# Keeping one expert pass in SBUF in place of two: the pass ahead of the last goes to DRAM by a scatter

## The chip, the cores and the metric

The kernel runs on one core of one Trainium2 chip. The metric is the device time of one launch in microseconds (us). The core has a matrix engine (PE, TensorE), a vector engine (DVE, VectorE), a scalar engine (ACT, ScalarE), GpSimd (POOL) and a queue engine (SP, SyncE); DMAs are issued from SP, ACT and POOL and share 16 DMA engines.

## What is computed

One inference step of a decoder layer for 512 prompt tokens and 8 sample tokens, 1024 wide. A pooling and mLSTM mixer and a cross-attention come first. The change concerns only the last step, a mixture of 16 gated-MLP experts, two for each token, and the last layer norm:

```python
hg = jnp.einsum('nd,edf->nef', xf, p['w_gate'])
hu = jnp.einsum('nd,edf->nef', xf, p['w_up'])
hh = jax.nn.silu(hg) * hu * combine[..., None]
y = jnp.einsum('nef,efd->nd', hh, p['w_down'])
...
x = layer_norm(ALPHA * x + hier_moe(x, p), p['ln3_g'], p['ln3_b'])
```

`combine` has two nonzero entries for each token (top expert group, then the top two of its four experts), so 520 tokens make 1040 rows of expert work.

## The kernel before

**Passes.** The 1040 rows are sorted by expert into 12 passes (`NPASS`) of 128 slots. Three experts (`FIRST`) have a pass each; the other 13 are ordered by their count of tokens, the fullest first, and share nine passes in groups of 32 slots. A slot holds a token's number, its gate and the row of `y_d` to which its result belongs (`entry(p)`). With the given inputs the counts leave 109, 95, 60, 98, 87 and 59 used slots in passes 6 to 11 (counted from the reference's routing and the table `GROUPS`).

**One pass.** POOL gathers the rows of its tokens from DRAM, PE turns them (L1125), multiplies by gate and up weights (L1144), turns the hidden rows (L1151) and multiplies by the down weights (L1164). DVE and ACT scale the two halves of the result by the gate and write it to `ysb`, a ring of three slots (DVE L2571, ACT L1749). PE's stream is laid so that the down products of pass p-1 come behind the gate and up products of pass p. SP streams the weights.

**Where a result goes.** For the first `NSCAT` = 10 passes POOL then scatters the 128 rows to `y_d` in DRAM by an indirect DMA (`scatter`, L2921). `y_d` has two halves, one for each token's first choice and one for its second. The last `KEPT` = 2 passes, 10 and 11, are not scattered: DVE builds for each a 0/1 matrix `places` of slots against tokens (`place_rows`, L2577 to L2581), and PE multiplies it with `ysb` (`add_kept` L1182 for the prompt, `add_samples` L1186 for the samples), so that the sums stand in PSUM by token.

**The end.** When all scatters have landed (`y_out`), POOL adds the rows of `y_d` to the residual `xn` by accumulating DMAs: `accumulate` (L2958) for the first choice of the samples and of prompt tiles 0, 1 and 2, then, behind waits, the second choice of the samples, the first of tile 4, and the second of tiles 2 and 4. SP loads the second choice of tiles 0 and 1 plainly into a weight buffer (L1352), and DVE adds it (L2598, two adds, ahead of everything that follows on DVE), each when its tile's two transfers have landed. Then DVE walks over the tiles in the order 0, samples, 1, 2, 4 (`LAST_NORM`): it adds the PSUM sums of the kept passes (L2625, two halves), takes the mean (L2630) and centres (L2632); ACT takes the squares and scales (L1784 to L1790), and POOL sends the tile out by an accumulating DMA (L2974). The last tile is finished by DVE (L2643) and sent by SP and ACT (L1358, L1793).

Every engine works its stream in order. What holds the scatters back from the accumulates is this wait on POOL, and the same on SP ahead of L1352:

```python
for i in range(3):
    pool.wait_ge(y_out[i], 16 * SCATTERS[i])
```

In the rows below `P` is the large SBUF buffer in which `ysb`, the centred tiles and others lie, `smp` holds `places` and the slot lists, `wring` and `mkT`/`mv` are weight buffers, and `ps` is PSUM.

Of the kernel before, what the change touches and what calls it, by code (L numbers as in the profile page):

```python
# [67 lines left out]
NSORT = NE - NFULL  # L68
RELEASE = [max(p for p in range(NPASS) if any(part[0] == n for part in PASS[p])) for n in range(NE)]
KCOL = NPASS - NFULL  # L70
KEPT = 2
NSCAT = NPASS - KEPT
SCATTERS = [len(range(i, NSCAT, 3)) for i in range(3)]
LW = 3
# [52 lines left out]
def layer_kernel(nc, a, o):  # L127
# [3 lines left out]
    with ctx:  # L131
# [3 lines left out]
        def sem(name):  # L135
            return ctx.enter_context(nc.semaphore(name))
# [46 lines left out]
        ps = [ctx.enter_context(nc.psum_tensor(f"ps{i}", [128, 512], F32)) for i in range(8)]  # L183
# [5 lines left out]
        def view(lo, n, pat=None, **kw):  # L189
            v = P[:, lo:lo + n]  # L190
            return v.rearrange(pat, **kw) if pat else v
# [83 lines left out]
        zeros = view(16094, 256)  # L275
        places = smp[:, 1120:1120 + KEPT * NTOK].rearrange("p (i c) -> p i c", i=KEPT)
        tokens16 = smp[:, 2162:2162 + KEPT]
        squares = view(10464, D)
# [3 lines left out]
        kept_bank = lambda t, q: 2 * PROMPT.index(t) + q  # L282
# [91 lines left out]
        y_act, y_dve = sem("y_act"), sem("y_dve")  # L374
        y_out = [sem(f"y_out{i}") for i in range(3)]
        sum_full, row_parts = sem("sum_full"), sem("row_parts")
# [21 lines left out]
        def wcols(w, c0, n=512):  # L398
# [8 lines left out]
                  ("wq0", wcols(a["ca_wq"], 0)), ("wq1", wcols(a["ca_wq"], 512)),  # L407
                  ("wc0", wcols(a["ca_wo"], 0)), ("wc1", wcols(a["ca_wo"], 512))]
        BI = {name: i for i, (name, _) in enumerate(BLOCKS)}
        NB = len(BLOCKS)  # L410
        assert NB % WR == 0
# [76 lines left out]
        def _(pe):  # L488
# [692 lines left out]
            def add_kept(i, bank, t, q, **open_close):  # L1181
                return mm(bank[:, :], places[:, i, START[t]:START[t] + TR], ysb[:, (NSCAT + i) % 3, q * 512:q * 512 + 512], **open_close)  # L1182

            def add_samples(i, bank):
                for g in range(4):
                    last = mm(bank[32 * g:32 * g + NS, 0:256], places[:, i, NP_:NTOK], ysb[:, (NSCAT + i) % 3, g * 256:g * 256 + 256],  # L1186
                              start=(i == 0), stop=(i == KEPT - 1))
                return last

            pe.wait_ge(places_ready, KEPT)  # L1190
            pe.wait_ge(y_act, NSCAT + 1)
            pe.wait_ge(y_dve, NSCAT + 1)
            add_samples(0, ps[6])
            add_kept(0, ps[0], 0, 0, start=True, stop=False)
            pe.wait_ge(y_act, NPASS)
            pe.wait_ge(y_dve, NPASS)
            for t in PROMPT:
                if t == 4:
                    pe.wait_ge(y_act, NPASS + 1)
                    pe.wait_ge(y_dve, NPASS + 1)  # L1200
                for q in range(2):
                    bank = ps[kept_bank(t, q)]
                    if (t, q) != (0, 0):
                        add_kept(0, bank, t, q, start=True, stop=False)
                    add_kept(1, bank, t, q, start=False, stop=True).then_inc(sum_full, 1)
                if t == 0:
                    add_samples(1, ps[6]).then_inc(sum_full, 1)

            with pe.If(over > 0):
                with pe.Fori(0, NE) as e:  # L1210
# [603 lines left out]
        def _(dve):  # L1814
# [749 lines left out]
            def expert_out(p):  # L2564
                dve.wait_ge(y_full, p + 1)
                if p >= 3:
                    dve.wait_ge(y_out[p % 3], 16 * (p // 3))
                elif p == 2:
                    dve.wait_ge(c_out, 32)
                dve.wait_ge(*entry_landed(p))  # L2570
                V.tensor_scalar(ysb[:, p % 3, 512:D], ps[5][:, :], entry(p)[:, 1:2], None, ALU.mult).then_inc(y_dve, 1)  # L2571

            def place_rows(i):
                p = NSCAT + i
                dve.wait_ge(*entry_landed(p))
                number = tokens16[:, i:i + 1]
                link(V.tensor_copy(number, entry(p)[:, 0:1].bitcast(U32)))  # L2577
                link(V.tensor_scalar(number, number, float(NE), None, ALU.mult))
                for t in range(NT):
                    n = rows_of(t)  # L2580
                    last = V.tensor_scalar(places[:, i, START[t]:START[t] + n], slots16[:, 0:n], number, -float(NE * START[t]), ALU.subtract, ALU.is_equal)  # L2581
                last.then_inc(places_ready, 1)

            for p in range(NPASS):
# [5 lines left out]
                if p > 0:  # L2590
                    expert_out(p - 1)
                if NPASS - 4 <= p < NPASS - 4 + KEPT:
                    place_rows(p - NPASS + 4)
# [426 lines left out]
```

## Time and profile before

| | us |
|---|---|
| median of 3 runs (lowest, highest) | 658.12 (658.09, 659.34) |
| the profiled execution | 657.6 |
| its span, first to last instruction | 655.9 |
| passes 9 to 11, each | about 11.7, the last shorter |
| result of the last scattered pass (9) in SBUF | at 612.94 |
| its scatter landed | at 618.90 |
| result of pass 10, of pass 11 in SBUF | at 624.44, 629.31 |
| first add of the last norm on DVE | at 632.51 |

Times "at" are microseconds from the start of the span. What stands outside the span is 657.6 - 655.9 = 1.7 us. The rows are read as a chain: the instruction that ended last, what released it, and so back. Busy shares alone (PE 95%) do not tell what the end of the program waits for.

### The profile page before, as it was taken

What the parts mean: (1) busy time and instruction counts of PE and PEld (TensorE: products, weight loads), DVE (VectorE), ACT (ScalarE), POOL (GpSimd) and SP (SyncE); (2) the same over time, 40 slices, a digit from 0 to 9 for tenths busy, and PEclk for the clock granted to TensorE, in tenths of its full rate; (3) what the DMA queues carried; (4) which work ended last, traced back from release to release, by engine and by line L of the source; (5) the groups of instructions that cost most, each with busy time, mean ns of one, the idle gap of its engine ahead of it and who ended that gap; (6) DMA issues with size and microseconds to landing.
All of it is one profiled execution on the core that took longest, in us unless ns stands there. A gap on an engine that the chain in (4) does not pass through costs nothing.

```text
span 655.9 us, 8866 instructions
## 1 busy us (share of the span) xinstructions
PE 625.2 (95%) x3279; PEld 399.9 (61%) x3279; DVE 365.5 (56%) x832; ACT 166.2 (25%) x371; POOL 205.7 (31%) x249
## 2 busy tenths in 40 slices
PE   6999999999999979999999999999999999999992
PEld 3588788887788844447888764454664454333330
DVE  1576797327646844557544865356864233253466
ACT  1184301102553120002003630223414111211144
POOL 7140100101667645212003983103234432111221
PEclk9999999999999989999999999999999999999997
DMA  8994588706355244005606886557638999999797
GB/s 280 364 371 139 191 196 233 252 2 210 115 164 193 94 176 146 16 1 205 243 6 230 327 270 262 224 204 282 253 126 352 415 411 415 403 375 414 271 178 158
DMA packets 49430, 150.29 MB, mean 229 GB/s; under 512 B 5691, under 2 KB 8459, under 8 KB 45153
## 3 DMA queue, kind: packets, MB, share of 16 engines
q1 hardware_dynamic: 35159, 112.48, 45.7%
q0 software_dynamic: 11488, 31.97, 17.2%
q10 hardware_dynamic: 2738, 5.23, 2.1%
q8 instruction: 28, 0.46, 0.3%
q14 instruction: 17, 0.14, 0.1%
HBM read 132.38 MB, written 22.43 MB: 236 GB/s over the span
## 4 chain that ended last, share of the span: by engine, by line
PE 77%; DMA 8%; DVE 7%; ACT 2%; POOL 2%; SPq 2%; issue 2%; DVEq 0%; POOLq 0%; ACTq 0%
PE ps L610 14%; PE ps L787 14%; PE ps L1144 12%; PE ps L608 7%; PE ps L516 5%; PE ps L1164 5%; DMA xn<-in_x_sample 2%; PE ps L806 2%; PE ps L889 2%; DMA xn<-y_d 2%; PE ps L1125 1%; PE ps L873 1%; PE ps L1016 1%; PE ps L583 1%; DMA wring<-in_ca_wq 1%
## 5 line engine op out<-in xcount | busy, mean ns | idle before, releaser
L787 PE MATMUL ps<-wring,P 128*128 128x512 f32 x224 | 99.2, 596 | 0.0
L787 PEld LDWEIGHTS ps<-wring,P 128*128 128x128 f32 x224 | 41.6, 190 | 49.1 <-issue 49.0
L1916 DVE SCALAR_TENSOR_TENSOR P<-ps,P 128x256 f32<-128x256 f32 (+1 forms) x83 | 33.7, 424 | 57.3 <-PE ps L610 36.6
L1144 PE MATMUL ps<-wring,P 128*32 128x512 f32 (+1 forms) x288 | 63.6, 593 | 0.9 <-DVE P L2549 0.9
L516 PE MATMUL ps<-xT,wring 128*128 128x312 f32 (+1 forms) x256 | 57.4, 383 | 0.0
L516 PEld LDWEIGHTS ps<-xT,wring 128*128 128x128 f32 x256 | 46.4, 190 | 9.3
L2549 DVE COPY P<-ps 128x512 f32<-128x512 f32 x11 | 7.6, 692 | 73.5 <-PE ps L1125 73.5
L1144 PEld LDWEIGHTS ps<-wring,P 128*32 128x32 f32 (+1 forms) x288 | 21.6, 128 | 35.0 <-issue 34.9
L2723 POOL TENSOR_SCALAR rstd<-agg 128x1 f32<-128x1 f32 (+1 forms) x10 | 12.0, 1196 | 88.0 <-DVE agg L1846 88.0
L2871 POOL TENSOR_TENSOR P<-P,xT 128x2048 f32<-128x2048 f32 x8 | 36.1, 4524 | 9.0 <-DMA xT<-sq_d 5.2
L2224 DVE SCALAR_TENSOR_TENSOR xn<-xn,ps 128x512 f32<-128x512 f32 x16 | 11.0, 685 | 44.9 <-PE ps L787 32.0
L1164 PE MATMUL ps<-P 128*32 128x512 f32 (+1 forms) x144 | 32.6, 594 | 0.6 <-issue 0.6
L608 PE MATMUL ps<-wring,P 128*128 128x256 f32 x128 | 29.5, 380 | 1.2 <-DVE wring L1891 1.2
L610 PE MATMUL ps<-xT,wring 128*128 128x264 f32 (+1 forms) x128 | 29.7, 387 | 0.2 <-DMA wring<-in_ca_wq 0.2
L610 PE MATMUL ps<-P 128*128 128x264 f32 x128 | 29.5, 385 | 0.0
L610 PE MATMUL ps<-P,wring 128*128 128x256 f32 (+1 forms) x128 | 29.2, 382 | 0.0
L1144 PE MATMUL ps<-xT,P 128*32 128x512 f32 (+1 forms) x96 | 28.2, 593 | 0.0
L610 PEld LDWEIGHTS ps<-xT,wring 128*128 128x128 f32 x128 | 23.8, 190 | 5.1 <-issue 1.1
L608 PEld LDWEIGHTS ps<-wring,P 128*128 128x128 f32 x128 | 23.8, 190 | 5.0 <-DVE wring L1891 1.6
L610 PEld LDWEIGHTS ps<-P 128*128 128x128 f32 x128 | 24.3, 190 | 4.2
L1469 ACT ACTIVATE xT<-ps 128x512 f32<-128x512 f32 (+1 forms) x20 | 9.5, 515 | 67.4 <-PE ps L583 67.3
L610 PEld LDWEIGHTS ps<-P,wring 128*128 128x128 f32 x128 | 24.2, 190 | 3.8
(464 smaller groups left out, 1171.6 us busy)
## 6 DMA issues: line engine op xcount, KB each, us to landing
wring<-in_w_in SPq DMA_DIRECT2D x5, 2048.0 KB, 9.8
wring<-in_w_gate SPq DMA_DIRECT2D x10, 1024.0 KB, 8.8
wring<-in_w_up SPq DMA_DIRECT2D x10, 1024.0 KB, 12.7
P<-in_w_down SPq DMA_DIRECT2D x10, 1024.0 KB, 13.5
P<-in_cache_mem_k SPq DMA_DIRECT2D x8, 1024.0 KB, 7.0
P<-in_cache_mem_v SPq DMA_DIRECT2D x8, 1024.0 KB, 6.1
y_d<-P POOLq DMA_DIRECT2D x1, 4160.0 KB, 31.6
wring<-in_ca_wv SPq DMA_DIRECT2D x2, 2048.0 KB, 20.4
```

The source lines that it names most:

```text
L516: last = mm(out, lhs(k), rhs(k), start=(k == 0), stop=(k == n - 1))
L608: last = mm(bank[:, 0:n], x[:, k, 128 * i:128 * i + 128], w[:, k, :], start=(k == 0), stop=(k == 3))
L610: last = mm(bank[:, 0:n], w[:, k, 128 * i:128 * i + 128], x[:, k, :], start=(k == 0), stop=(k == 3))
L787: last = mm(bk[:, :], src[:, k, START[t]:START[t] + TR], w[:, k, :], start=(k == 0), stop=(k == KC - 1))
L806: last = mm(bank[:, :], mixT[:, k, 0:TR], w[:, k, :], start=(k == 4), stop=(k == 1))
L889: last = mm(bk[:, 0:cn], mv[:, m, h * CE + ec * 128:h * CE + ec * 128 + 128], paT[:, h, m, c0:c0 + cn], start=(m == 0), stop=(m == 1))
L1144: last = mm(GU[p % 2][lo:lo + m, :].rearrange("p (g f) -> p g f", g=2), xgT[:, p % 3, k, lo:lo + m], gu[s][:, :, k, :], start=(k == 0), st ...
L1164: last = mm(YB[q][lo:lo + m, :], hT[:, p % 2, f, lo:lo + m], dn[s][:, f, q * 512:q * 512 + 512], start=(f == 0), stop=(f == 1))
L1916: V.scalar_tensor_tensor(dst, src, scale, part, ALU.mult, ALU.add).then_inc(part_added, 1)
L2224: V.scalar_tensor_tensor(x, x, ALPHA, bk[:, :], ALU.mult, ALU.add).then_inc(dve_free, 1)
L2723: link(G.tensor_scalar(x, agg[0:n, 1:2], LN_EPS, None, ALU.add))
L2871: G.tensor_tensor(x, x, qb[:, b % 4:b % 4 + 1].broadcast_to([128, 2, D]), ALU.mult).then_inc(kq_done, 1)
```

## The change

`KEPT` falls from 2 to 1, so `NSCAT` rises from 10 to 11 and `SCATTERS` from [4, 3, 3] to [4, 4, 3]. Pass 10 is scattered by POOL like the passes ahead of it, and the waits of POOL and SP on all scatters now count that one too. `places` is built for pass 11 alone, and PE's products for pass 10 are gone, with the first wait and the products that stood ahead of the wait for pass 11.

```diff
-KEPT = 2
+KEPT = 1
 NSCAT = NPASS - KEPT
 SCATTERS = [len(range(i, NSCAT, 3)) for i in range(3)]
...
             pe.wait_ge(places_ready, KEPT)
-            pe.wait_ge(y_act, NSCAT + 1)
-            pe.wait_ge(y_dve, NSCAT + 1)
-            add_samples(0, ps[6])
-            add_kept(0, ps[0], 0, 0, start=True, stop=False)
             pe.wait_ge(y_act, NPASS)
             pe.wait_ge(y_dve, NPASS)
             for t in PROMPT:
...
                 for q in range(2):
-                    bank = ps[kept_bank(t, q)]
-                    if (t, q) != (0, 0):
-                        add_kept(0, bank, t, q, start=True, stop=False)
-                    add_kept(1, bank, t, q, start=False, stop=True).then_inc(sum_full, 1)
+                    add_kept(0, ps[kept_bank(t, q)], t, q, start=True, stop=True).then_inc(sum_full, 1)
                 if t == 0:
-                    add_samples(1, ps[6]).then_inc(sum_full, 1)
+                    add_samples(0, ps[6]).then_inc(sum_full, 1)
```

On POOL, the stream from the last gather (L2887, L2880 after: lines below the edit move up by 7) to the accumulates. Before:

```order
L2921 DMA y_d<-P,smp 1040x1024
L2887 DMA P<-x_d,smp 128x1024
L2921 DMA y_d<-P,smp 1040x1024 x4
L2951 TENSOR_LOAD flag
L2951 ISA x2
L2958 DMA xn<-y_d 8x1024
L2958 DMA xn<-y_d 128x1024 x3
```

and after:

```order
L2914 DMA y_d<-P,smp 1040x1024
L2880 DMA P<-x_d,smp 128x1024
L2914 DMA y_d<-P,smp 1040x1024 x5
L2944 TENSOR_LOAD flag
L2944 ISA x2
L2951 DMA xn<-y_d 8x1024
L2951 DMA xn<-y_d 128x1024 x3
```

One scatter more stands in a row ahead of the first accumulate; nothing else on POOL has moved.

On PE, the end of the stream, behind the down products of pass 11 (L1164):

```order
 L1164 MATMUL ps<-mv,P 32x512 x2
 L1164 MATMUL ps<-P 32x512 x2
+L1182 MATMUL ps<-P,smp 128x512 x2
 L1186 MATMUL ps<-P,smp 8x256 x4
-L1182 MATMUL ps<-P,smp 128x512 x4
-L1186 MATMUL ps<-P,smp 8x256 x4
-L1182 MATMUL ps<-P,smp 128x512 x12
```

```order
+L1182 MATMUL ps<-P,smp 128x512 x6
```

Sixteen products for the prompt tiles became eight, eight for the samples became four, and those of tile 0 now stand ahead of the samples'.

## Rows read from the trace of the kernel before

**Rows 1.** The page: the span and the busy time of each engine.

```profile
span 655.9 us, 8866 instructions
PE 625.2 (95%) x3279; PEld 399.9 (61%) x3279; DVE 365.5 (56%) x832; ACT 166.2 (25%) x371; POOL 205.7 (31%) x249
```

**Rows 2.** The chain that ended last, 608 to 635: start, length, what (us).

```profile
608.55 3.61 PE ps L1164 x32
...
612.19 0.76 DVE P L2571
...
614.21 4.70 DMA y_d<-P,smp
...
619.47 1.27 POOL xn L2958 x2
620.74 10.61 DMA xn<-y_d
...
632.51 0.68 DVE xn L2625
```

**Rows 3.** Timeline of POOL: start, length, what, [idle before <-what ended it].

```profile
619.47 3.66 POOL L2958 DMA_DIRECT2D xn<-y_d  x4 [4.28 <-DMA y_d<-P,smp]
...
634.09 0.84 POOL L2958 DMA_DIRECT2D xn<-y_d  x1 [7.59 <-DMA xn<-y_d]
636.90 0.84 POOL L2958 DMA_DIRECT2D xn<-y_d  x1 [1.97 <-DMA xn<-y_d]
```

**Rows 4.** Timeline of DVE, from the last `place_rows` to the last tile.

```profile
601.54 1.01 DVE L2581 TENSOR_SCALAR smp<-con,smp 128x128 f32<-128x128 f32 x5
...
623.69 0.75 DVE L2571 TENSOR_SCALAR P<-ps,smp 128x512 f32<-128x512 f32 x1 [1.22 <-PE ps L1164]
628.56 0.75 DVE L2571 TENSOR_SCALAR P<-ps,smp 128x512 f32<-128x512 f32 x1 [4.12 <-PE ps L1164]
629.23 1.22 DVE L2598 TENSOR_TENSOR xn<-xn,wring 128x1024 f32<-128x1024 f32 x1
631.37 1.22 DVE L2598 TENSOR_TENSOR xn<-xn,wring 128x1024 f32<-128x1024 f32 x1 [0.93 <-DMA xn<-y_d]
...
642.22 0.68 DVE L2625 CUSTOM_DVE_ANT_0 xn<-xn,ps 128x512 f32<-128x512 f32 x1
...
645.06 0.68 DVE L2625 CUSTOM_DVE_ANT_0 xn<-xn,ps 128x512 f32<-128x512 f32 x1
```

**Rows 5.** Timeline of PE: the products of the kept passes (records, two for each 128x512 product).

```profile
632.49 0.62 PE L1186 MATMUL ps<-P,smp 128*8 128x256 f32 x8
...
633.04 10.57 PE L1182 MATMUL ps<-P,smp 128*128 128x512 f32 x24
```

**Rows 6.** DMA of the stretch 614.2 to 619: bytes by queue, and issues with their landing.

```profile
q1 hardware_dynamic: 259, 1.00, 53.4%
q0 software_dynamic: 144, 0.40, 20.8%
...
y_d<-P,smp POOLq DMA_INDIRECT x1, 4.7
```

**Rows 7.** The gather of pass 1 (L2887, 486 to 488, other DMA share 0.01).

```profile
L2887 POOL DMA_INDIRECT P<-x_d,smp x1: 1058/1058/1058, 486.6 to 486.6; - x1
...
DMA to landing us min/median/max: 4.4/4.4/4.4
```

**Rows 8.** The scatter at 590.6: DMA of 590.6 to 599, weights streaming beside it.

```profile
DMA packets 591, 3.42 MB, mean 408 GB/s; under 512 B 96, under 2 KB 96, under 8 KB 252
...
y_d<-P,smp POOLq DMA_INDIRECT x1, 9.4
```

**Rows 9.** DMA of 619 to 624.7, the accumulates beside SP's loads.

```profile
DMA packets 356, 1.23 MB, mean 216 GB/s; under 512 B 56, under 2 KB 56, under 8 KB 356
```

**Rows 10.** DMA of 624.7 to 631.4, the accumulates alone.

```profile
DMA packets 364, 1.37 MB, mean 205 GB/s; under 512 B 32, under 2 KB 32, under 8 KB 363
...
q0 software_dynamic: 363, 1.36, 104.8%
```

## The prediction

> **What bounds the kernel now.** I began with the page: PE is busy for 95% of the span [rows 1], which would suggest that taking products off PE helps. That share is an average, so I read the end of the program in the chain that ended last [rows 2]. Up to the down products of pass 9 the chain runs on PE. Then it leaves PE for good, although two passes are still to come: DVE finishes the result of pass 9, which ends at 612.94; POOL begins the scatter at 614.21; it lands 4.70 later, at 618.91; POOL issues the accumulates from 619.47; and the transfer behind the second of the issues in the chain lands at 620.74 + 10.61 = 631.35. What it releases is seen in the timeline of DVE [rows 4]: the second add of L2598 starts at 631.37, after DVE stood idle for 0.93 us until "DMA xn<-y_d". From there the last norm runs without a break on DVE to the last tile. So the kernel ends on a chain of transfers that starts with the last *scattered* pass, and passes 10 and 11 are computed beside it. Their results come at 623.69 + 0.75 = 624.44 and 628.56 + 0.75 = 629.31 [rows 4], the second 2.1 us ahead of the add at 631.37. The order of these two ends, 631.37 for the transfers and 629.31 + 1.22 for pass 11 and the first add, is what the change touches.
>
> **The change part by part.**
>
> *The scatter of pass 10 (added, on the path).* POOL stands idle when this scatter could start, since nothing else is in its stream; but behind it on POOL stand all the accumulates, and on SP the two loads of second choices wait for the same landing. The scatter can start only when pass 10's result is in SBUF. The last scatter's source is thus ready at 624.44 in place of 612.94, which is **+11.50 us** [rows 2, 4]. From source to start of the transfer before were 614.21 - 612.94 = 1.27 us, and I take the same.
>
> *How long that scatter takes.* The scatter of pass 9 took 4.7 us, and 1.00 MB of weights moved beside its 0.40 MB [rows 6]. Pass 10 has 87 rows in place of 98, and no weights are left to load. The trace shows no scatter alone. Bound below: the weights' 1.00 MB, at the 408 GB/s at which a full stream moves [rows 8], is 2.5 us of the engines' time, and if all of it was taken from the scatter, 4.7 - 2.5 = 2.2 us remain. Bound above: 9.4 us, beside a full stream of weights [rows 8]. The nearest row is the gather of pass 1, another indirect DMA of POOL, issued when the DMA engines were empty: 4.4 us for 58 rows [rows 7]. I take 4.4, so **-0.3 us**, and keep 2.2 to 9.4 for the range, far nearer to the lower end, because the stream of weights that makes the upper end is over.
>
> The Trainium skill bears on this ("DMA: Bandwidth & Descriptors", section "Anatomy of one DMA — SWDGE (gpsimd) path"): it gives about 2.0 us fixed plus the bytes at 436 GB/s. For 87 rows of 4 KB that would be an estimate of 2.8 us, and the sum would be 1.6 us smaller. The gather of pass 1, with fewer bytes, took 4.4 us in this trace, so I stay with the row.
>
> *From the landing to the second add (moved as a whole).* Before, from 618.91 to 631.37, 12.46 us [rows 2, 4]. These are the issues on POOL, SP's two loads, and accumulates that then fill the DMA engines by themselves: 104.8% of 16 engines on POOL's queue, with nothing on SP's or ACT's [rows 10]. Nothing that runs beside them slows them there, so moving them to a quieter time gives nothing. The start is different: four issues took 3.66 us, where single ones later took 0.84 [rows 3], so 4 x 0.84 = 3.36 and up to 0.3 us might come back, with DVE idle by then. As the engines are full behind it, I take **0** and keep -0.3 for the range.
>
> On this too the Trainium skill has a rule ("SBUF — State Buffer", the warning on the "DVE blocks DMA" trap): a vector operation in a two-port mode keeps GpSimd from writing descriptors. After the change DVE would be idle at that moment, so by that rule the 0.3 us would be had; it is inside the range.
>
> *The tail behind the second add (moved as a whole).* Its order on DVE, ACT and POOL is unchanged, and no part of it has another release before than after: DVE's own order is the path, and the late accumulates of tiles 2 and 4 are issued at 634.09 and 636.90 [rows 3], 8.1 us ahead of DVE's need at 642.22 and 645.06 [rows 4], where DVE shows no idle time before it; both shift with the rest. **0**.
>
> *Products off PE (removed, off the path).* 24 records took 10.57 us [rows 5], 0.44 each, two to a product, so eight products are 7.0 us, and the samples' eight records 0.3 to 0.6 more. Before, the last sum was ready at 633.04 + 10.57 = 643.61; the last tile's first half is added at 645.06 and its second half 0.68 later, so PE was ahead. After, from 629.31: two products 1.8, samples 0.6, six products 5.3, so about 637.0. Tile 0's sums are then ready at some 631.1, and DVE wants them only at about 643.7. **0**. What hid them was the transfer chain; that cover becomes larger.
>
> *One `place_rows` off DVE (removed).* Its five comparisons take 1.01 us [rows 4], with two smaller operations ahead of them about 1.4, at 601.2 to 602.6, while DVE's next work waits for PE. **0**. The remaining one, for pass 11, is built one pass earlier than pass 11's was; its slot list was loaded long before.
>
> *The sum.* 11.50 - 0.3 = **+11.2 us**. The span goes from 655.9 to 667.1, the profiled execution from 657.6 to 668.8, and against the median of the runs, 658.12, which is 0.5 above the profiled one, to **669.3 us**, slower by 1.7%.
>
> **The rivals.**
>
> *A. The scatter and accumulates run markedly faster when alone.* In the 12.4 us between 619.0 and 631.4, 1.23 + 1.37 = 2.60 MB were moved, the second part at 205 GB/s [rows 9, 10]. If contention with the matrix stream or the loads had halved the rate, and all of it could run at the 408 GB/s of [rows 8], the stretch would take 6.4 us instead of 12.5 and give back 6: 669.3 - 6 = 663.3. Against: the 104.8% share is POOL's queue alone [rows 10]. It says that accumulating transfers take that long by themselves. Chance 0.05.
>
> *B. The scatter takes as long as the earlier ones,* 9.4 us [rows 8], because its time lies in the indirect writes to DRAM and not in the weights beside it: +5.0 over my 4.4, so 674.3. Against: pass 9's took 4.7 as the weights ran out. Chance 0.04.
>
> *C. Not slower: PE's sums, not the transfers, release the last norm.* The place would be DVE's first add of sums (L2625 at 632.51). Were it held by PE, the halved products would be worth up to 6.6 us (643.61 to 637.0), and the time would be as low as 651.5. It decides only if the accumulates land before pass 11's sums are ready, at 631.1; for that the last scatter would have to land 12.5 us earlier, at 618.6, while its source is ready at 624.44. DVE also shows "DMA xn<-y_d" and never "PE" as what ended its idle time in the tail [rows 4]. Chance 0.01.
>
> *D. The change does not do what it says,* for instance POOL's wait not counting the new scatter, with which nothing would move: 658.1. `SCATTERS` is derived from `NSCAT`, and the stream shows the fifth scatter ahead of the accumulates. Chance 0.01.
>
> **How the numbers follow.** The forecast, +11.2 with the chain moved whole, has 0.89; A 0.05, B 0.04, C 0.01, D 0.01. The range comes from the forecast's own unknowns: below, a scatter of 2.2 us in place of 4.4 and 0.3 from the issues give 666.8, of which I leave out the last few tenths; above, a scatter of about 5.3 and the spread of the runs (659.34 against 658.12) give 671.4, trimmed to 671.0. So 667.1 to 671.0. This kernel's measurement tells about 0.2% from no change, 1.3 us. Faster by over that 0.01 (C), within it 0.01 (D), slower 0.98.
>
> **What the profile after would show.** The scatter of pass 10 starts at about 625.7 and lands at about 630.1. The first accumulate is issued at about 630.7, where it was 619.47. DVE's two adds of L2598 (L2591 after) start late, the second at about 642.6 behind an idle time that "DMA xn<-y_d" ended, of which a part of the wait now stands ahead of the first add. The first add of sums comes at 643.7 and PE's last product ends at about 637, so PE is idle for the last 30 us. The stretch from the landing to the second add stays at 12.2 to 12.5 us, and from there to the end of the span at 24.5. If the landing comes before 629 the -0.3 was too small; if the stretch of 12.5 shrinks, A is at work; if DVE waits for PE anywhere behind 632, C. The forecast would be wrong altogether if the accumulates were issued before pass 10's scatter has landed.

## The result

The changed kernel took 667.09 us (median of 4 runs, 665.57 to 667.52), the kernel before 658.38 (median of 4, 658.09 to 659.34). The ratio is 1.0129 with a 95% interval of 1.0105 to 1.0153: slower by 1.3%, or 8.7 us between the medians. Forecast were +11.2 us and 669.3, with 667.1 to 671.0. The direction and the mechanism were right; the cost was sized too high, and the median lies 0.01 us below the forecast range. The profiled execution of the changed kernel took 665.57 us, the lowest of its four, with a span of 663.7.

The page after, to be read against [rows 1]:

```profile
span 663.7 us, 8813 instructions
PE 619.5 (93%) x3255; PEld 397.0 (60%) x3255; DVE 365.2 (55%) x825; ACT 166.1 (25%) x371; POOL 205.9 (31%) x250
```

PE has 5.7 us less to do and the program is longer. The chain that ended last (start, length, what), against [rows 2]:

```profile
622.95 0.76 DVE P L2564
...
623.83 0.52 issue
624.34 0.21 POOLq L2944
624.55 3.22 DMA y_d<-P,smp
...
628.42 1.27 POOL xn L2951 x2
629.69 9.45 DMA xn<-y_d
...
640.31 0.68 DVE xn L2618
```

It now leaves PE one pass later, at pass 10, and then has the same links: DVE's result, the scatter, the issue of accumulates, the landing of tile 1. Lines below the edit carry numbers lower by 7.

DVE's timeline (start, length, what, [idle before <-what ended it]), against [rows 4]:

```profile
611.45 0.75 DVE L2564 TENSOR_SCALAR P<-ps,smp 128x512 f32<-128x512 f32 x1
...
622.95 0.75 DVE L2564 TENSOR_SCALAR P<-ps,smp 128x512 f32<-128x512 f32 x1 [1.22 <-PE ps L1164]
627.82 0.75 DVE L2564 TENSOR_SCALAR P<-ps,smp 128x512 f32<-128x512 f32 x1 [4.12 <-PE ps L1164]
636.22 1.23 DVE L2591 TENSOR_TENSOR xn<-xn,wring 128x1024 f32<-128x1024 f32 x1 [7.65 <-DMA xn<-y_d]
639.16 1.23 DVE L2591 TENSOR_TENSOR xn<-xn,wring 128x1024 f32<-128x1024 f32 x1 [1.72 <-DMA xn<-y_d]
```

Where DVE had waited 0.93 us for transfers, it now waits 7.65 + 1.72 = 9.37 us. From the second add to the end of the span are 663.7 - 639.16 = 24.54 us, against 655.9 - 631.37 = 24.53 before.

POOL, against [rows 3]:

```profile
628.42 3.66 POOL L2951 DMA_DIRECT2D xn<-y_d  x4 [2.90 <-DMA y_d<-P,smp]
633.94 1.69 POOL L2951 DMA_DIRECT2D xn<-y_d  x2 [1.85 <-DMA xn<-y_d]
641.96 0.84 POOL L2951 DMA_DIRECT2D xn<-y_d  x1 [6.34 <-DMA xn<-y_d]
```

PE's products of the kept pass, against [rows 5]:

```profile
628.72 1.95 PE L1182 MATMUL ps<-P,smp 128*128 128x512 f32 x4 [0.96 <-DVE P L2564]
630.60 0.62 PE L1186 MATMUL ps<-P,smp 128*8 128x256 f32 x8
631.15 3.70 PE L1182 MATMUL ps<-P,smp 128*128 128x512 f32 x8
644.21 3.75 PE L1182 MATMUL ps<-P,smp 128*128 128x512 f32 x4 [9.35 <-DVE P L2629]
```

**The two spans, term by term.** Forecast and measured, between the two profiled executions:

| term | forecast | measured |
|---|---|---|
| work ahead of pass 9's result, not touched | 0 | -0.74 (pass 9's result begins at 611.45 against 612.19) |
| result of pass 9 to result of pass 10 | +11.50 | +11.50 |
| result to start of the scatter | 0 | 0.85 against 1.27: -0.42 |
| the scatter | -0.3 | 3.22 against 4.70: -1.48 |
| landing to the issue of accumulates | 0 | 0.65 against 0.56: +0.09 |
| that issue to the second add | 0 | 10.74 against 11.90: -1.16 |
| second add to the end | 0 | +0.01 |
| sum | +11.2 | +7.8 |

The untouched part varies from run to run by more than this 0.74: DVE begins the result of pass 11 anywhere between 627.2 and 633.2 us in ten traces of this case. So in the experiments traces are compared from that point (called "pass 11's result" below), not from the start.

### The profile page after: what moved, and what is told of

The parts are those of the page before. It is cut to its first block, busy times and chain, and to the rows that moved or that the text cites. A ratio compares the mean times of both kernels' runs of the same rounds, so it can differ in the third digit from the quotient of the medians.

```text
span 663.7 us, 8813 instructions
## 1 busy us (share of the span) xinstructions
PE 619.5 (93%) x3255; PEld 397.0 (60%) x3255; DVE 365.2 (55%) x825; ACT 166.1 (25%) x371; POOL 205.9 (31%) x250
## 4 chain that ended last, share of the span: by engine, by line
PE 79%; DVE 7%; DMA 6%; ACT 2%; POOL 2%; SPq 2%; issue 2%; DVEq 0%; POOLq 0%; ACTq 0%
PE ps L610 15%; PE ps L787 14%; PE ps L1144 13%; PE ps L608 7%; PE ps L1164 6%; PE ps L516 5%; DMA xn<-in_x_sample 2%; PE ps L806 2%; PE ps L889 2%; PE ps L583 2%; PE ps L873 1%; PE ps L1125 1%; PE ps L1016 1%; DMA xn<-y_d 1%; SPq L1262 1%
## 5 line engine op out<-in xcount | busy, mean ns | idle before, releaser
L2716 POOL TENSOR_SCALAR rstd<-agg 128x1 f32<-128x1 f32 (+1 forms) x10 | 11.9, 1195 | 87.4 <-DVE agg L1839 87.4
L1164 PE MATMUL ps<-P 128*32 128x512 f32 (+1 forms) x144 | 32.6, 594 | 0.6 <-issue 0.6
L2914 POOL DMA_INDIRECT y_d<-P,smp x11 | 11.1, 1010 | 57.2 <-DVE P L2564 32.5
```

Of the source, the lines that this page charges most:

```text
L1164: last = mm(YB[q][lo:lo + m, :], hT[:, p % 2, f, lo:lo + m], dn[s][:, f, q * 512:q * 512 + 512], start=(f == 0), stop=(f == 1))
L2716: link(G.tensor_scalar(x, agg[0:n, 1:2], LN_EPS, None, ALU.add))
```

## The experiments

**Is it the landing of the last scatter, and that alone?** The change has two sides, an added scatter and removed products; each was made alone. Without the addition:

```diff
-SCATTERS = [len(range(i, NSCAT, 3)) for i in range(3)]
+SCATTERS = [len(range(i, NSCAT - 1, 3)) for i in range(3)]
...
-                if 0 <= p - 5 < NSCAT:
+                if 0 <= p - 5 < NSCAT - 1:
```

> Pass 10 is neither scattered nor added by products: its result is left out of the output. Everything else is the changed kernel. It is the change's removals (products, one place_rows) without its addition. If the last scatter's landing sets the end: the time of the kernel before, 658 us within 1, and DVE's second add of L2591 at about 631. If PE's products also held the end: up to 1 us below the kernel before. If the cost lay in something else than the scatter's wait, such as the order of PE's stream: above 660.

Measured: 659.06 us (median of 10), ratio to the kernel before 1.0017 (0.9992 to 1.0042). The removals, pass 10 left out altogether, are worth nothing that can be measured. Its chain and DVE's adds:

```profile
616.29 4.91 DMA y_d<-P,smp
```

```profile
630.64 0.75 DVE L2564 TENSOR_SCALAR P<-ps,smp 128x512 f32<-128x512 f32 x1 [4.12 <-PE ps L1164]
631.30 1.22 DVE L2591 TENSOR_TENSOR xn<-xn,wring 128x1024 f32<-128x1024 f32 x1
632.87 1.23 DVE L2591 TENSOR_TENSOR xn<-xn,wring 128x1024 f32<-128x1024 f32 x1 [0.35 <-DMA xn<-y_d]
```

The chain starts at pass 9 again, and DVE waits 0.35 us for it. Without the removals, in the kernel before:

```diff
-SCATTERS = [len(range(i, NSCAT, 3)) for i in range(3)]
+SCATTERS = [len(range(i, NSCAT + 1, 3)) for i in range(3)]
...
-                if 0 <= p - 5 < NSCAT:
+                if 0 <= p - 5 < NSCAT + 1:
```

> The kernel before, with pass 10 scattered in addition and the waits counting that scatter, while its products stay (its result is added twice, in the scatter and in the products). It is the addition without the removals. If the scatter's landing alone sets the end: as the changed kernel, 667 us within 1.5. Rival (the removed products gave something back): 1 to 7 us above the changed kernel, with DVE waiting for PE in the tail.

Measured: 666.94 us, ratio 1.0137 (1.0091 to 1.0182), as the changed kernel, whose second set of runs on that chip gave 1.0142. Chain, and DVE:

```profile
625.90 3.51 DMA y_d<-P,smp
```

```profile
638.39 1.23 DVE L2598 TENSOR_TENSOR xn<-xn,wring 128x1024 f32<-128x1024 f32 x1 [8.46 <-DMA xn<-y_d]
640.85 1.23 DVE L2598 TENSOR_TENSOR xn<-xn,wring 128x1024 f32<-128x1024 f32 x1 [1.23 <-DMA xn<-y_d]
```

So the added scatter with the wait for it is the whole cost, and the products beside it are free to keep or to drop. Both halves show that. The scatter and its wait were added together; that the wait carries the cost is read from the rows, where the accumulates are issued 0.65 us behind the landing, after POOL stood idle for it.

**Why did the scatter take 3.2 us and not 4.7?** Either the weights beside pass 9's scatter or its 98 rows against 87. In the changed kernel SP issues one more load when the down products of pass 10 are done:

```diff
+            sp.wait_ge(y_full, NPASS - 1)
+            sp.wait_ge(gu_full, NPASS)
+            sp.dma_start(gu[2][:, 0], one_expert(gate_w, 0)).then_inc(gu_in[2], 16)
```

> The changed kernel, with one more load of 512 KB of weights into a buffer nobody reads, issued by SP when pass 10's down products are done, about when its scatter starts. If weights beside it made pass 9's scatter long (4.7 us beside 1.00 MB, against 3.2 alone): the scatter takes 3.9 to 4.7 us, the time up by 0.7 to 1.5. If the difference lay in the number of rows (98 and 87): 3.2 us, no change.

The load is twice as large as the text on record says, 1.05 MB, as the DMA view of 622 to 629.9 shows:

```profile
q1 hardware_dynamic: 144, 1.05, 38.4%
q0 software_dynamic: 144, 0.36, 11.7%
```

The chain, where the scatter takes 5.17 us:

```profile
624.69 5.17 DMA y_d<-P,smp
630.51 1.27 POOL xn L2954 x2
```

Measured: 668.33 us (1.015, 1.0114 to 1.0185); from pass 11's result to DVE's last operation 30.70 us, against 28.74 and 28.79 in the two traces of the changed kernel. The 1.95 us that the scatter lost arrive at the end in full. The number of rows was the same in both, so the load beside it alone makes a scatter of 87 rows longer by 1.95 us, more than the 1.48 us to be explained. What the 11 rows more of pass 9 cost by themselves was not tried.

**Is the stretch of accumulates shorter because the other engines are quiet?** Theory S on record says that this stretch varies by itself, rival Q that quiet surroundings shorten it. Second traces of both kernels, unedited:

> The changed kernel once more, unedited, for a second trace. Theory S (the gains of the scatter and of its start are fixed, the stretch behind it is not): source to start about 0.9 us, scatter 3.2 us, landing to second add of L2591 anywhere from 11.4 to 12.5 us; the span then about 664 to 665. Rival Q (the accumulates run faster because the other engines are quiet beside them): the stretch is 11.4 us again, within 0.2.

> The kernel before once more, unedited, for a second trace. Theory S: scatter of pass 9 4.7 us again, landing to second add (L2598) anywhere from 11.4 to 12.5. Rival Q: that stretch is 12.5 again, within 0.2.

The changed kernel again: 666.47 us (1.0142, 1.0098 to 1.0186), with a scatter of 3.25 us, and

```profile
629.23 3.66 POOL L2951 DMA_DIRECT2D xn<-y_d  x4 [2.93 <-DMA y_d<-P,smp]
```

```profile
640.00 1.23 DVE L2591 TENSOR_TENSOR xn<-xn,wring 128x1024 f32<-128x1024 f32 x1 [1.27 <-DMA xn<-y_d]
```

that is 10.77 us from the issue to the second add, and 11.42 from the landing, which fits S and Q alike. The kernel before again (one run, 661.62 us, late by about 4.6 us ahead of the part that matters):

```profile
624.11 3.66 POOL L2958 DMA_DIRECT2D xn<-y_d  x4 [4.28 <-DMA y_d<-P,smp]
...
637.63 0.84 POOL L2958 DMA_DIRECT2D xn<-y_d  x1 [5.40 <-DMA xn<-y_d]
```

```profile
633.21 0.75 DVE L2571 TENSOR_SCALAR P<-ps,smp 128x512 f32<-128x512 f32 x1 [4.12 <-PE ps L1164]
633.88 2.35 DVE L2598 TENSOR_TENSOR xn<-xn,wring 128x1024 f32<-128x1024 f32 x2
...
637.25 0.69 DVE L2625 CUSTOM_DVE_ANT_0 xn<-xn,ps 128x512 f32<-128x512 f32 x1 [0.42 <-PE ps L1182]
```

This trace changes the reading of [rows 4]. DVE's two adds run in one piece here: tile 1 had landed by 635.1, within 11.0 us of the issue, where Q asked for 11.9 again, and the wait of 0.93 us is absent. Instead DVE waits 0.42 us for PE's sums. The trace on which the prediction was built had the longest such stretch of those in the table below. The landing of tile 2's first transfer is seen in every trace, as the start of POOL's first single issue. The kernels are named by their edits here: the second traces end in again, no_scatter and both are the two halves above, load_beside has the added load, pe_running, add_late and add_early follow below.

| kernel | issue to second add | issue to tile 2 landed | pass 11's result to DVE's last |
|---|---|---|---|
| before | 11.90 | 14.62 | 20.20 |
| before_again | no wait | 13.52 | 19.69 |
| no_scatter | 11.11 | 13.82 | 19.62 |
| after | 10.74 | 13.54 | 28.74 |
| after_again | 10.77 | 13.53 | 28.79 |
| both | 10.79 | 13.53 | 29.06 |
| pe_running | 10.92 | 13.69 | 28.91 |
| load_beside | 10.76 | 13.49 | 30.70 |
| add_late | add moved | 13.64 | 28.20 |
| add_early | add moved | 14.12 | 20.60 |

And with PE kept busy while the accumulates run, by products into a bank that is overwritten:

```diff
                 if t == 4:
+                    keep_running(ps[kept_bank(4, 1)], 16)
                     pe.wait_ge(y_act, NPASS + 1)
```

> The changed kernel, with 16 products of 336 columns added on PE behind the sums of tile 2, into the bank of tile 4's second half and overwritten by it, so that PE is busy while the accumulates run (about 9 us from 635). Rival Q (a quiet PE makes the accumulates faster): the stretch from landing to second add goes from 11.4 to 12.5 us, the time up by 1. Theory S: no change beyond the spread, 667 us. The products of tile 4 run at full clock and end about 2 us earlier than in the changed kernel, which frees nobody.

Measured: 667.45 us (1.0142, 1.0104 to 1.0181), the stretch 10.92 us, not 12.5.

```profile
636.78 9.20 PE L1039 MATMUL ps<-con 128*128 128x336 f32 x32
646.47 1.96 PE L1182 MATMUL ps<-P,smp 128*128 128x512 f32 x4 [0.49 <-DVE P L2630]
```

A PE busy in the second half of the stretch does not lengthen it. For a quieter place there is this: the four traces with the stretch in its old place show 13.52, 13.82, 14.12 and 14.62 us to tile 2, the six in the new place 13.49 to 13.69. So up to about half a microsecond on average may belong to the place; DVE and ACT, which work on pass 11 beside the stretch in its old place, were not tried, and what made the 14.62 stays open.

**The other side: one pass more kept.** Passes 9, 10 and 11 are added by products:

```diff
-KEPT = 2
+KEPT = 3
...
-            add_samples(0, ps[6])
-            add_kept(0, ps[0], 0, 0, start=True, stop=False)
+            for i in range(2):
+                add_samples(i, ps[6])
+                add_kept(i, ps[0], 0, 0, start=(i == 0), stop=False)
...
+                        add_kept(1, bank, t, q, start=False, stop=False)
-                    add_kept(1, bank, t, q, start=False, stop=True).then_inc(sum_full, 1)
+                    add_kept(2, bank, t, q, start=False, stop=True).then_inc(sum_full, 1)
```

> One pass more is kept instead of one less: passes 9, 10 and 11 are added by products, 9 passes are scattered. The last scatter then starts at 602, the accumulates at about 611, and both walls trade places: PE needs 24 products for the prompt tiles, the last sum comes at about 650 against 643.6 before. Theory (the end is the later of two chains, transfers and products): slower than the kernel before by 2 to 4 us, 660 to 662, with DVE waiting for PE in the tail. Rival (the transfer chain is the only one): faster, by up to 1 us, since DVE's second add starts at once after the result of pass 11.

Measured: 661.74 us (median of 9), 1.0056 (1.0035 to 1.0078), slower by 0.6%, or 3.9 us against the 657.80 of the kernel before in the same set. The theory held. DVE in the tail, and PE:

```profile
630.70 2.35 DVE L2600 TENSOR_TENSOR xn<-xn,wring 128x1024 f32<-128x1024 f32 x2
634.11 0.69 DVE L2627 CUSTOM_DVE_ANT_0 xn<-xn,ps 128x512 f32<-128x512 f32 x1 [1.05 <-PE ps L1182]
...
636.54 0.69 DVE L2627 CUSTOM_DVE_ANT_0 xn<-xn,ps 128x512 f32<-128x512 f32 x1 [1.74 <-PE ps L1182]
...
652.74 0.69 DVE L2627 CUSTOM_DVE_ANT_0 xn<-xn,ps 128x512 f32<-128x512 f32 x1 [1.69 <-PE ps L1182]
```

```profile
636.98 15.72 PE L1182 MATMUL ps<-P,smp 128*128 128x512 f32 x36
```

The transfers are early and DVE does not wait for them, although tile 2's first one took 17.6 us from the first issue (613.29 to 630.91), with SP's last load of weights beside it. PE's last sum comes at 652.7, and DVE waits for PE at both halves of tile 0 and again later. With three passes kept PE's products set the end, with one the transfers do. With two the ends meet: of the two traces of the kernel before, one has 0.93 us of waiting for transfers, the other 0.42 us for PE.

**Can the new wait be covered?** In the changed kernel DVE's add for tile 1 is moved from ahead of the last norm to its own tile:

```diff
-            for t in (0, 1):
+            def add_choice(t):
                 dve.wait_ge(x3_in[t], 16)
...
+            add_choice(0)
...
+                if t == 1:
+                    add_choice(1)
```

> The changed kernel, with DVE's add of the second choice of tile 1 moved from ahead of the whole last norm to just ahead of tile 1's part of it. In the changed kernel DVE waits 1.3 to 1.7 us for that tile's transfers while tile 0 is ready. Theory (transfers of tile 0 and then DVE's own order set the end): the first add of sums starts right after the first add of L2591, about 1.3 to 1.7 us earlier, and the time is 1.3 to 1.7 us below the changed kernel's, some 665.5. Rival (the later accumulates of tiles 2 and 4 bind next): DVE waits for them, and less than 0.5 us is left.

Measured: 665.94 us (median of 6, 663.53 to 669.80), 1.0139 (1.0103 to 1.0174), which the runs cannot tell from the changed kernel. DVE:

```profile
636.34 1.23 DVE L2591 TENSOR_TENSOR xn<-xn,wring 128x1024 f32<-128x1024 f32 x1 [8.41 <-DMA xn<-y_d]
637.70 0.69 DVE L2621 CUSTOM_DVE_ANT_0 xn<-xn,ps 128x512 f32<-128x512 f32 x1
...
641.91 0.68 DVE L2621 CUSTOM_DVE_ANT_0 xn<-xn,P 8x512 f32<-8x512 f32 x1 [0.45 <-DMA xn<-y_d]
```

The wait for tile 1 is gone, but neither expectation held. The first sum starts at once as hoped; then the samples' second transfer, which stands behind the others, is late by 0.45 us. Tile 0's transfers were later too: DVE stood 8.41 us for them, against 7.65 and 8.15 in the two unedited traces. These two waits took back more than half of the 1.3 to 1.7 us. From pass 11's result (627.18) to DVE's last (655.38) are 28.20 us, 0.5 to 0.6 less than unedited.

The same move in the kernel before, with tile 0's add ahead of the result of pass 11 as well:

```diff
             dve.wait_ge(xa_ready, NT)
+            add_choice(0)
+            expert_out(NPASS - 1)
```

> The kernel before, with the same move of tile 1's add, and tile 0's add ahead of the result of pass 11 on DVE, where DVE waits 4.1 us for PE. Tile 0's transfers land about 8.3 us after the first accumulate's issue, just about when the result of pass 11 is due. Theory (the kernel before is bound by the result of pass 11 and DVE's order behind it): up to 0.9 us faster than the kernel before, 657.2 to 658. Rival (tile 0 lands later than pass 11's products, so its add holds them up): 0 to 1 us slower.

Measured: 658.14 us (median of 12), 1.0014 (0.9990 to 1.0038): no gain.

```profile
627.06 1.23 DVE L2597 TENSOR_TENSOR xn<-xn,wring 128x1024 f32<-128x1024 f32 x1 [3.21 <-DMA xn<-y_d]
628.20 0.74 DVE L2571 TENSOR_SCALAR P<-ps,smp 128x512 f32<-128x512 f32 x1
630.43 0.69 DVE L2628 CUSTOM_DVE_ANT_0 xn<-xn,ps 128x512 f32<-128x512 f32 x1 [1.48 <-PE ps L1182]
...
632.01 0.69 DVE L2628 CUSTOM_DVE_ANT_0 xn<-xn,ps 128x512 f32<-128x512 f32 x1 [0.88 <-PE ps L1182]
```

The add fits into DVE's wait but for about 0.2 us: the result of pass 11 begins 5.11 us behind that of pass 10, against 4.87 in the kernel before. What the move saved turns into 1.48 + 0.88 us of waiting for PE's sums of tile 0.

## Why the prediction was right or wrong

**Right: what ends the program.** The chain from the last scattered pass through its landing to tile 1's add moved as a whole. The 11.50 us between the two results was exact, the tail behind the second add kept its length to 0.01 us, and the two halves of the change made alone gave 1.0137 for the addition and 1.0017 for the removals. Rivals C and D fell with that, and B with the scatter of 3.2 us. The sign that the prediction gave for a scatter sized too long, a landing before 629, came: 627.77. The signs named for the right case were there: the scatter ahead of the accumulates, both DVE waits on "DMA xn<-y_d", PE idle for a long time.

**Wrong: "I take 4.4, so -0.3 us" for the scatter.** It took 3.22, 3.25 and 3.22 us without weights beside it (3.51, also without, in the kernel that kept both sets of products; why stays open). The row taken as the nearest was the wrong one. The gather of pass 1 reads DRAM by rows, and it was not alone for long: POOL issued a second gather 1.36 us behind it and a first scatter of slot lists at 489.34, and the four list scatters landed after 3.2 us in the median. The scatter of pass 9 was the same operation, and what was needed was its price without 1.00 MB of company: between the 0.3 us that I took off and the bound of 2.5, it was 1.5. The lower bound of 2.2 us misses the measured 3.22 by 1.0, the value taken by 1.2. This is 1.2 us of the miss. The Trainium skill's fit for such a DMA ("DMA: Bandwidth & Descriptors", "Anatomy of one DMA — SWDGE (gpsimd) path") gave 2.8 us for the 87 rows: 0.4 below the measured 3.22, where my row was 1.2 above.

**Wrong: "I take the same" for 1.27 us from source to start.** It is 0.85 for pass 10 in all traces of kernels that scatter it, and 1.27 or 1.28 for pass 9 in the traces looked at (in the changed kernel 612.20 to 613.48). That is 0.42 us of the miss. Why the two differ was not tried.

**Wrong: "From the landing to the second add" as a constant.** I took one trace's 12.46 us as the price. In the changed kernel's own it is 11.39, of which 10.74 from the issue, and the other traces lie nearer to the short value. This is 1.1 us of the miss between the two profiled executions. Rival A named the quieter surroundings; the busy PE of one experiment and the 13.52 us to tile 2 in the second trace of before speak against them as the main cause. With the same short stretch the kernel before is not held by transfers at all but by pass 11's result and PE's sums, so that this shortening is for the most part not a gain of the change: in the second trace of before DVE ends 19.69 us behind pass 11's result, against 28.77 after (mean of two traces), a difference of 9.1. Taken from the first trace it is 28.77 - 20.20 = 8.6. The median difference is 8.7, which is 2.5 below the forecast 11.2. The scatter and its start, 1.6 us together, recur in every trace; the other 0.9 lie in this stretch and in the spread of the runs, and no run parts them further.

**Kept for the range, and not had: the 0.3 us for POOL's issues.** The four issues took 3.66 us before and 3.66 after, with DVE idle after. The rule on the "DVE blocks DMA" trap from the Trainium skill ("SBUF — State Buffer") thus had nothing here to give back. It speaks of vector operations in a two-port mode, and no row shows whether one of those beside the issues (619.48 to 622.47) ran in such a mode, so this is no test of it.

**Wrong without effect: PE's last product at 637.** The first half of tile 4's sums uses the bank in which the samples' sums stand, and `pe.wait_ge(y_act, NPASS + 1)` holds them until ACT and DVE have copied those. Before, PE came there late enough not to wait. After, it stood 9.35 us until DVE's copy (L2629) and ended at 647.96, 11 us later than forecast, still ahead of DVE's need. A step was left out there: of products that move ahead, each wait in PE's stream counts, too.

**Wrong: the range.** Its terms gave 666.8 at the lower end, and I cut 0.3 off; the median is 667.09. The spread of a single trace's stretch, 1.1 us here, had no place in it.

## What to carry to other kernels

Where transfers end the program, the last pass whose result goes through DRAM sets the end by the time its data are ready plus the whole round trip, here 0.85 + 3.2 + 0.65 + 10.7 us. Keep as many passes on chip as that trip covers and no more: in this kernel, with one too few the transfers bind (+8.7 us), with one too many the added products do (+3.9). A transfer's price is that of the same operation with its company of bytes taken off, and a stretch read from one execution needs a second before it enters a sum as a constant.

## What the runs showed of the hardware

An indirect scatter of 87 rows of 4 KB took 3.2 us alone (3.5 in one trace) and 5.2 beside one load of 1.05 MB that had been issued 1.6 us ahead of it (623.08 against 624.69).

TensorE's clock fell in PE's new idle time. The stretches 634.9 to 644.2 and 644.2 to 648 of the changed kernel (length, busy time of PE, PEld, DVE, ACT, POOL, granted clock, DMA share, GB/s):

```profile
634.90:644.20 9.30, 0.00 (x0) 0.03 (x1) 6.01 (x10) 1.53 (x3) 1.57 (x2) 0.72 1.03 192
644.20:648.00 3.80, 3.75 (x4) 1.15 (x4) 3.67 (x11) 2.61 (x5) 1.71 (x2) 0.50 1.00 162
```

Behind the idle stretch the four records of tile 4 ran at a granted clock of 0.50, the 1.2 GHz level, and took 3.75 us; with PE kept busy ahead of them they took 1.96 us at 1.00, the 2.4 GHz level. It cost nothing only because nobody waited for them: DVE read those sums from 652.85 on.
